# Second and third gate of a decoder trunk as seven products of half-size blocks

## What is computed

```python
b_ga, b_gb, b_gc = jnp.split(b_gate, N_BRANCH, axis=-1)
merged = (jax.nn.sigmoid(ga + b_ga) * jnp.einsum('bsw,wd->bsd', y_a, w_branch[0])
          + jax.nn.sigmoid(gb + b_gb) * jnp.einsum('bsw,wd->bsd', y_b, w_branch[1])
          + jax.nn.sigmoid(gc + b_gc) * jnp.einsum('bsw,wd->bsd', y_c, w_branch[2]))
mixed = jnp.einsum('bsd,de->bse', merged, w_o)
x = _layer_norm(ALPHA * x + mixed, ln1_g, ln1_b)
h = jnp.square(jax.nn.relu(jnp.einsum('bsd,df->bsf', x, w_up)))
x = _layer_norm(ALPHA * x + jnp.einsum('bsf,fd->bsd', h, w_down), ln2_g, ln2_b)
```

## Time and profile before

| | us |
|---|---|
| median of 3 runs | 835.32 (833.45 to 835.56) |
| the profiled execution | 836.42 |
| its span, first to last instruction | 834.6 |
| PE busy | 819.2 |
| DVE busy | 504.1 |
| ACT busy | 348.7 |
| POOL busy | 20.8 |
| the three gates, on PE | 252.09 to 447.93 |

### The profile page before, as it was taken

How to read it: one execution, slowest core, us unless ns; L and a number is a source line. 1 busy time by engine, 2 the same in 40 slices (tenths; PEclk the granted TensorE clock), 3 DMA queues, 4 the chain that set the end, 5 groups by cost and what they waited for, 6 DMA issues and landing times.

```text
span 834.6 us, 10182 instructions
## 1 busy us (share of the span) xinstructions
PE 819.2 (98%) x4111; PEld 695.7 (83%) x4111; DVE 504.1 (60%) x560; ACT 348.7 (42%) x393; POOL 20.8 (2%) x30
## 2 busy tenths in 40 slices
PE   8999999999999999999999999999999999999994
PEld 7989988889888888888888889888888888888883
DVE  3647735567364424414428685885669566947698
ACT  4539343484334223232225035653545345435430
POOL 1110100000001000000000010000000000000000
PEclk9999999999999999999999999999999999999998
DMA  9641313312212322323833407017301810270002
GB/s 304 201 152 52 101 51 97 105 50 83 68 66 90 117 82 100 101 101 101 302 101 99 153 7 247 0 51 252 102 0 53 301 51 0 84 270 1 0 1 101
DMA packets 68215, 87.52 MB, mean 105 GB/s; under 512 B 1581, under 2 KB 51798, under 8 KB 68182
## 3 DMA queue, kind: packets, MB, share of 16 engines
q1 hardware_dynamic: 68182, 87.06, 31.0%
HBM read 84.96 MB, written 2.10 MB: 104 GB/s over the span
## 4 chain that ended last, share of the span: by engine, by line
PE 94%; DVE 4%; issue 1%; DMA 1%; DVEq 0%; SPq 0%; ACT 0%
PE bank L1272 30%; PE bank L1274 30%; PE bank L1273 30%; DVE two L1172 1%; DVE two L1184 1%; DMA two<-in_mem_dram 1%; PE bank L1486 0%; PE bank L1436 0%; PE bank L1554 0%; PE bank L1407 0%; PE bank L1299 0%; DVE two L1189 0%; DVE w_lo L761 0%; DVE decay L1178 0%; DVE smx L1178 0%
## 5 line engine op out<-in xcount | busy, mean ns | idle before, releaser
L1272 PE MATMUL bank<-x_hi,w_hi 128*128 128x512 f32 (+1 forms) x704 | 268.4, 381 | 0.0
L1273 PE MATMUL bank<-x_lo,w_hi 128*128 128x512 f32 (+1 forms) x704 | 267.2, 380 | 0.0
L1274 PE MATMUL bank<-x_hi,w_lo 128*128 128x512 f32 (+1 forms) x704 | 267.2, 379 | 0.0
L756 DVE TENSOR_TENSOR w_lo<-raw,w_hi 128x2048 fp32r<-128x2048 f32 x40 | 91.5, 2291 | 107.7 <-ACT w_hi L474 107.5
L1274 PEld LDWEIGHTS bank<-x_hi,w_lo 128*128 128x128 f32 x704 | 132.4, 188 | 25.1
L1272 PEld LDWEIGHTS bank<-x_hi,w_hi 128*128 128x128 f32 x704 | 132.4, 188 | 24.6
L1273 PEld LDWEIGHTS bank<-x_lo,w_hi 128*128 128x128 f32 x704 | 132.5, 188 | 24.5
L1272 PE MATMUL bank<-w_hi,y_hi 128*128 128x512 f32 (+1 forms) x320 | 121.5, 380 | 0.4 <-DVE two L1172 0.4
L1274 PE MATMUL bank<-w_hi,y_lo 128*128 128x512 f32 (+1 forms) x320 | 121.1, 378 | 0.0
L1273 PE MATMUL bank<-w_lo,y_hi 128*128 128x512 f32 (+1 forms) x320 | 121.1, 378 | 0.0
L474 ACT ACTIVATE w_hi<-raw 128x2048 fp32r<-128x2048 f32 x40 | 76.4, 1915 | 41.7 <-PE bank L1274 36.8
(11 more groups left out here) (182 smaller groups left out, 834.2 us busy)
## 6 DMA issues: line engine op xcount, KB each, us to landing
raw<-in_w_in_dram SPq DMA_DIRECT2D x28, 1024.0 KB, 5.0
raw<-in_w_up_dram SPq DMA_DIRECT2D x16, 1024.0 KB, 8.8
small<-in_w_down_dram SPq DMA_DIRECT2D x12, 1024.0 KB, 7.0
raw<-in_w_branch_dram SPq DMA_DIRECT2D x6, 1024.0 KB, 5.1
raw<-in_w_o_dram SPq DMA_DIRECT2D x4, 1024.0 KB, 5.1
raw<-in_w_down_dram SPq DMA_DIRECT2D x4, 1024.0 KB, 4.7
two<-in_x_dram SPq DMA_DIRECT2D x2, 1024.0 KB, 11.0
small<-in_w_mem_v_dram SPq DMA_DIRECT2D x2, 1024.0 KB, 11.8
```

The costliest lines, as they stand in the source:

```text
L756: dve.tensor_tensor(w_lo[:, slot, :], raw[:, r, :], w_hi[:, slot, :].bitcast(F32), ALU.subtract)\
L1272: pe.matmul(dst, a[0], b[0], start=first, stop=False, skip_group_check=goes_on)
L1273: pe.matmul(dst, a[0], b[1], start=False, stop=False, skip_group_check=goes_on)
L1274: return pe.matmul(dst, a[1], b[0], start=False, stop=last, skip_group_check=goes_on)
```

## The change

The gates' loop is written out. The first gate is computed as before, in the order gate slabs 0 and 1, both branch slabs, gate slabs 2 and 3; its products open `merged`, so the clearing goes. The second and third gate (x times a 1024 x 1024 block) are each made of seven products m1 to m7, over half the tokens (256), half of the 1024 inputs (4 blocks) and half of the outputs (512). The operands are three blocks of x as they are (m1, m2, m4) and four sums of blocks (m5, m6, m7, m3), formed once by VectorE during the first gate and split into parts; and three blocks of weights as loaded (m1, m2, m3), with four sums (m5, m6, m4, m7), which VectorE forms in the raw buffers. The branch slabs come seventh and ninth in the order. The quarter results z11, z12, z22 are formed in SBUF from two or more products (ScalarE copies one out of PSUM, VectorE adds the next), while others accumulate in PSUM; z21 is read from PSUM.

Two more raw buffers lie over rows 0 to 3 of y_hi and y_lo, free once the first branch is used. Half results lie in rows 1, 2, 4 and 5 of `two`, sums of x in rows 0 and 3 of `two` and in small[:, 4096:9216].

The core of the diff, by engine. SyncE (`gate_load(i, name)` loads one slab of gate i, i = 3 is w_o; `split_of` waits until that slab's low part is made):

```diff
+            split_of(0, "g2")
+            gate_load(1, "m1")
+            split_of(0, "g3")
+            gate_load(1, "m2")
+
+            sp.wait_ge(tile_done, GATE_ROUND * MAIN + 12)
+            gate_load(1, "c")
+            gate_load(1, "m3")
+            split_of(1, "m6")
+            sp.wait_ge(gate_block_summed, block_summed(1, "m4"))
+            gate_load(1, "b1")
...
+            gate_load(3, 0)
+            split_of(2, "m7")
+            gate_load(2, "b0")
+            split_of(2, "m4")
+            gate_load(3, 1)
+            sp.wait_ge(slab_lo, S_OUT + 1)
+            gate_load(3, 2)
+
+            sp.wait_ge(merge_done, merged_at(2, KD - 1))
+            sp.wait_ge(gate_done, gate_made(2, "m4", 1))
             sp.dma_start(resid, x_t).then_inc(x_again, 16)
+            sp.wait_ge(slab_lo, S_OUT + 2)
+            gate_load(3, 3)
             for n, v in enumerate((ln1_g, ln1_b, ln2_g, ln2_b)):
                 sp.dma_start(ln_par[:, n, :], v.to_broadcast((P, D))).then_inc(ln_landed, 16)
-            for e in range(2):
-                for h in range(2):
-                    load(S_OUT + 2 * e + h, h, wout[:, 4 * h:4 * h + 4, e * WID:(e + 1) * WID], 4)
```

ScalarE (for i = 1, 2; `nexts(p)` is the slab four places on, `product(i, name)` waits until that product is made):

```diff
+                if i == 2:
+                    gate_hi(2, "m6", product(1, "b0"))
+                gate_copy(i, "m1", "z11", 1.0)
+                gate_hi(*nexts(1), product(i, "m1"))
+                gate_hi(*nexts(2), product(i, "m2"))
+                gate_opens(i, "z11")
+                gate_copy(i, "m5", "z22", 1.0)
+                gate_hi(*nexts(3), product(i, "m5"))
+                gate_copy(i, "m6", "z12", -1.0)
+                gate_hi(*nexts(4), product(i, "m6"))
+                gate_hi(*nexts(5), product(i, "m3"))
+                gate_opens(i, "z12")
+                gate_hi(*nexts(6), product(i, "m7"))
+                gate_opens(i, "z22")
+                gate_hi(*nexts(7), product(i, "b1"))
+                if i == 2:
+                    merged_parts(0)
+                gate_opens(i, "z21")
+                gate_hi(*nexts(8), product(i, "m4"))
             merged_parts(1)
-            hi(S_OUT + 3, 2, OUT_ROUND * MAIN)
+            gate_hi(3, 3, product(2, "b0"))
```

VectorE (for i = 1, 2):

```diff
+                gate_lo(i, "m6")
+                block_sum(i, "m4")
+                gate_lo(i, "m3")
+                block_sum(i, "m7")
+                gate_sums(i, "z11")
+                gate_lo(i, "m7")
+                gate_lo(i, "b1")
+                gate_lo(i, "m4")
+                gate_sums(i, "z12")
+                gate_lo(i, "b0")
+                gate_sums(i, "z22")
+                if i == 1:
+                    gate_lo(2, "m1")
+                else:
+                    gate_lo(3, 0)
+                gate_merge(i, 1)
+                if i == 1:
+                    gate_lo(2, "m2")
+                    block_sum(2, "m5")
+                    gate_lo(2, "m5")
+                    block_sum(2, "m6")
+                else:
+                    gate_lo(3, 1)
+                    merged_parts(0)
+                    gate_lo(3, 2)
+                gate_merge(i, 0)
             merged_parts(1)
-            lo(S_OUT + 2, 3)
-            lo(S_OUT + 3, 2)
+            gate_lo(3, 3)
```

TensorE (the order is LATER_GATE):

```diff
+LATER_GATE = ("m1", "m2", "m5", "m6", "m3", "m7", "b1", "m4", "b0")
...
+            def gate_product(i, name):
+                s = gate_slab(i, name)
+                slab(s)
+                if i == 1 and name in ("m6", "m7", "m5", "m3"):
+                    pe.wait_ge(x_sum_split, ("m6", "m7", "m5", "m3").index(name) + 1)
+                opens = name in ("m1", "m2", "m5")
+                for t in range(4):
+                    if t % 2 == 0:
+                        gate_ready(i, name, t // 2)
+                    for k in range(4):
+                        mm = three(gate_acc(name, t), w_part(s % 4, k * WID + t * P, P),
+                                   both(x_form_hi[name], x_form_lo[name], ALL, k), opens and k == 0 and t % 2 == 0,
+                                   k == 3, not opens or t % 2 == 1)
+                    if t % 2:
+                        mm.then_inc(gate_done, 1)
```

More of the change, by code:

```diff
@@ L352, in _ @@
                     load(half * N_PROJ + (S_PROJ + j), j % 2, win_256[:, :, ds(n, 1), :], KD)
-            with sp.Fori(0, 3) as i:
-                for h in range(2):
[L355 to L359, removed]
@@ L606, in _, with gate_hi @@
                         .then_inc(hgrn_hi, 1)
[L609 to L629, removed]
+            def gate_hi(i, name, earlier):
+                earlier()
+                if i == 3:
+                    s, p, src = S_OUT + name, OUT_PLACE[name], name
+                    act.wait_ge(place_landed[p], landing(3, name))
+                else:
+                    s = gate_slab(i, name)
+                    if i == 0 or name in ("m1", "m2", "m3", "b1", "b0"):
+                        p = place_of(i, name)
+                        act.wait_ge(place_landed[p], landing(i, name))
+                    else:
+                        p = PLACE[i][dict(m5="m1", m6="m1", m4="m2", m7="m3")[name]]
+                        act.wait_ge(gate_block_summed, block_summed(i, name))
+                act.activation(w_hi[:, s % 4, :], gate_raw[p], ACT.Copy).then_inc(slab_hi, 1)
@@ L639, in _ @@
-            gates(2, True)
-            hi(S_OUT + 2, 3)
+            gate_hi(0, "b0", tiles(-2))
+            gate_hi(0, "b1", tiles(0))
+            act.wait_ge(branch_split, 8)
+            first_opens(0)
+            first_opens(1)
+            gate_hi(0, "g2", tiles(2))
+            x_sum_high("m6", 1)
+            first_opens(2)
+            first_opens(3)
+            gate_hi(0, "g3", tiles(4))
+            x_sum_high("m7", 2)
+            x_sum_high("m5", 2)
+            gate_hi(1, "m1", tiles(8))
@@ L1003, in _, with gate_lo @@
                 assert chain[0] == CHAIN_HALF, chain
[L1006 to L1024, removed]
+            def gate_lo(i, name):
+                if i == 3:
+                    s, p = S_OUT + name, OUT_PLACE[name]
+                else:
+                    s = gate_slab(i, name)
+                    p = place_of(i, dict(m5="m1", m6="m1", m4="m2", m7="m3").get(name, name))
+                dve.wait_ge(slab_hi, s + 1)
+                low_of(w_lo[:, s % 4, :], gate_raw[p], w_hi[:, s % 4, :]).then_inc(slab_lo, 1)
@@ new lines, in gate_merge @@
+            def gate_merge(i, f):
+                for c in range(4):
+                    k = 4 * (1 - f) + c
+                    row = merged[:, k, :].rearrange("p (a t) -> p a t", a=2)
+                    g = gate_tile(f, c)
+                    dve.wait_ge(gate_opened, opened(i, "z22" if f else "z21", c))
+                    dve.wait_ge(gate_done, gate_made(i, "b%d" % f, c))
+                    src = bank[BRANCH_BANK[c]].rearrange("p (a t) -> p a t", a=2)
+                    dve.tensor_tensor(g, g, src, ALU.mult).then_inc(branch_read, 1)
+                    if i == 1 and k < 4:
+                        main_copied(dve, GATE_ROUND, 4 + k)
+                    else:
+                        dve.wait_ge(merge_done, merged_at(i - 1, k))
+                    dve.wait_ge(branch_read, KD * (i - 1) + k + 1)
+                    dve.tensor_tensor(row, row, g, ALU.add).then_inc(merge_done, 1)
@@ L1094, in _ @@
                 if b == TB - 1:
-                    lo(S_MLP, 0)
-                    lo(S_MLP + 1, 1)
+                    for n in (S_MLP, S_MLP + 1):
+                        dve.wait_ge(slab_hi, n + 1)
+                        low_of(w_lo[:, n % 4, :], raw[:, n % 2, :], w_hi[:, n % 4, :]).then_inc(slab_lo, 1)
                 mixed(b, 1)
@@ L1511, in _, with first_gate @@
                 feature_tile(rnd, 15, 3, 1)
[L1513 to L1530, removed]
+            def first_gate(name):
+                s = gate_slab(0, name)
+                slab(s)
+                n = int(name[1])
+                if name[0] == "g":
+                    t0 = 2 * n if n < 2 else 12 + 2 * (n - 2)
+                    for c in range(2):
+                        feature_tile(GATE_ROUND, t0 + c, s % 4, c)
+                    return
+                pe.wait_ge(branch_split, 8)
+                for c in range(4):
+                    dst = begin(GATE_ROUND, 4 + 4 * n + c)
+                    for k in range(HEADS):
+                        mm = three(dst, w_part(s % 4, k * WID + c * P, P), both(y_hi, y_lo, ALL, k),
+                                   k == 0, k == HEADS - 1)
+                    mm.then_inc(tile_done, 1)
@@ new lines, in branch_product @@
+            def branch_product(i, f):
+                s = gate_slab(i, "b%d" % f)
+                slab(s)
+                for c in range(4):
+                    if f == 0:
+                        pe.wait_ge(branch_read, KD * (i - 1) + c + 1)
+                    elif BRANCH_BANK[c] < 2:
+                        pe.wait_ge(gate_summed, summed(i, "z11", BRANCH_BANK[c]))
+                    elif i == 1:
```

(7 more changed lines are left out.)

307 lines of the change are left out of this document (279 added, 28 removed).

## The result

| | before | changed |
|---|---|---|
| median of 20 runs, us | 835.08 | 836.51 |
| lowest to highest | 833.45 to 836.38 | 835.04 to 838.66 |
| profiled execution | 836.42 | 835.04 |
| its span | 834.6 | 833.1 |

The ratio is 1.0022, 95% interval 1.0015 to 1.0028. So the changed kernel is slower by 0.22%. That is less than the 0.3% that the prediction takes for no change, though the interval excludes 1. Forecast: 836.2.

The account below looks back on a forecast made before the run. TensorE's stream of matmuls was taken as the bound (PE busy 819.2 of 834.6 us). 836.42 - 6.40 (gates) + 5.5 (stall) + 1.8 (clock) = 837.3, less 1.10 gives 836.2 us; range 831.5 to 839.5.

Parts of the forecast that it names:

- Rate of 256-token matmuls: Later two gates: 256-token matmuls take 0.120 us each, so each gate saves 3.2 us, 6.4 us together.
- The Trainium skill's formula: Isolated matmul gap of N/2.4 + 2.5 ns; would save 9.5 us in two gates; the prediction used the trace's figures instead.
- VectorE's and ScalarE's new work is hidden: Later gates: VectorE 44.9 us and ScalarE 27.5 us in 62.1 us, costed at nothing, as is the first gate's extra work.
- the edge at the refill of the weight slots: Later gates: refilling a slab's slot has 17.3 us of cover and needs 12.0 us at worst.
- What is late next: After the gates: x issued at 443.4 behind the last merge, fourth w_o slab behind it; PE stands still 5.5 us.
- No second wait: First layer norm: x1 ready some 7 us after the ln loads; PE first asks 11 us after the stall's end.
- The clock: Behind the w_o stall: clock falls from 2.4 to 1.2 GHz, costing 1.8 us, bounds 0 and 2.4.
- The 4 us at the lower level: Start of trace: 256-token matmuls 0.213 us apart instead of 0.120 for some 4 us, used to price the clock's fall.
- the even choice that 0.36 against 0.28 made of it: Stall of 4 to 7 us at the w_o slab: chance 0.36 with the clock's fall, 0.28 without.
- the w_o slab did not share the engines with x: Rival, load not late enough: slab shares with x, lands about 2.5 us sooner, stall 3.0 us, 831.9 us; chance 0.14.
- the loads did not crawl: Rival: x load and slab behind it at 290 GB/s, stall 8.7 us, clock down 1.8, 839.4 us; chance 0.14.
- the gates did not starve: Rival in the gates: late z sum on VectorE holds PE, a few us per event; chance 0.08 together with slow matmuls.

Follow-up runs that it names:

- e8: Changed kernel with fourth w_o slab, ln vectors and two rows of x loaded early, plus four extra VectorE passes per later gate: 828.65 us, 0.9926 to before.
- e6: e1 with VectorE making the low part twice for all nine slabs of each later gate: 836.29 us, ratio 1.0011 to the kernel before.
- e1: Changed kernel with the fourth w_o slab loaded once its raw buffer is free, ahead of the last-merge wait: 827.62 us, ratio 0.9917 to before.
- e2: Changed kernel with the fourth w_o slab ahead of x, both still behind the last merge: 832.28 us, ratio 0.9966 to the kernel before.
- e10: The changed kernel itself, unaltered, measured again beside the early-slab version on one chip: 837.04 us, ratio 1.0031 to the kernel before.
- e4: Kernel before, gates untouched, with x, the fourth w_o slab and the ln vectors moved behind the last merge: 845.22 us, ratio 1.0115.

## Why the prediction was right

The sum came out term by term, the clock's term partly by luck.
- *Rate of 256-token matmuls.* 0.120 us forecast, gates of 62.12 us found: the saving is 6.3 us, 6.4 forecast. The Trainium skill's formula (TensorE: Matmul & The Clock Gate, section Back-to-back issue gap), which would have given 9.5, is not borne out by this kernel either.
- *VectorE's and ScalarE's new work is hidden.* VectorE 42.6 to 43.5 us busy per later gate, 44.9 forecast, no PE gap; e8 shows it with 9 us more, e6 where it ends. The prediction looked for the edge at the refill of the weight slots. The one that e6 found is a hand-over out of PSUM, the copy of m5, which the prediction took for safe because a copy is short: ScalarE makes it in order, behind work that waits for VectorE. In the changed kernel it was done at 394.63 for a use at about 399.6.
- *What is late next.* The last merge ended 1.75 us after the gates (1.68 forecast) and x was issued 1.78 us after them (1.9), slab at hand 10.6 after the x issue (10.2), stop 5.75 (5.5).
- *No second wait.* Right for the changed kernel. But the some 4 us to spare (ready 7 us after the ln loads, wanted 11 us after the stall; 3.3 us in the profile, x1 ready at 464.86 and wanted at 468.21) belong to a kernel that has just stood still. Once the stall is gone (e1) it is 0.5 us, and in e2 it is gone.
- *The clock.* The size was right, 1.97 against 1.8, but the argument for it was weaker than it looked. The 4 us at the lower level came from the start of the trace, where the earlier trace rows show only matmuls of 256 tokens; PE also ran eight transposes ahead of them in 1.57 us, 0.2 us each (the changed kernel's profile has the same eight in 0.79 us), and the clock column reads 1.00 there, so the level is read from the rate alone. Behind the stops the time was 4.0 us here, 3.1 in e10 and 6.2 in e4, so that 4 is one value of several. Whether it would fall rested on one figure, the 5.2 us between the last matmul and the fall at the end of the trace, just under the stop of 5.5. In one profile the fall came 2.95 us into the stop, in e10 only 0.3 us before its end; but of the 26 measured executions of the changed kernel all but one have a mean granted clock of 0.993 or less, and that one has 0.994. So it was not the even choice that 0.36 against 0.28 made of it.

The rivals: the w_o slab did not share the engines with x (e2: swapped, it came 5 us sooner), the loads did not crawl in the changed kernel, though in e4 they took 1.4 us more, and the gates did not starve.

## What to carry to other kernels

When a change reuses buffers, list what was loaded into them early and ask for each load what now stands ahead of it in its queue. Here a slab whose own buffer was free 14 us sooner (e1 issues it at 426.51, the changed kernel at 440.88) was late only because it stood behind a wait and a load that it did not need; that order cost 7.7 us, more than seven products for eight saved. And price a stop of TensorE at more than its length: where the clock fell with it, these runs paid 1.3 to 3 us on top.

## What the runs showed that was not expected

**How soon the clock falls.** Stops and falls, in us: changed kernel, stop at 449.56, fall 2.95 later; e4, stop at 457.91, fall 3.1 later; e2, stop at 463.83, fall 2.5 later; e6, stop at 401.31, fall 4.7 later. The changed kernel's second profile (e10) stopped at 449.77 for 5.76 us, and there the clock held almost until PE began again:

```profile
454.00:455.00 1.00, 0.00 (x0) 0.00 (x0) 1.00 (x1) 0.45 (x1) 0.00 (x0) 1.00 1.03 422
455.00:456.00 1.00, 0.47 (x1) 0.47 (x2) 0.47 (x1) 0.00 (x0) 0.00 (x0) 0.62 0.57 234
...
458.00:459.00 1.00, 1.00 (x5) 0.77 (x4) 0.28 (x1) 0.00 (x0) 0.00 (x0) 0.68 0.95 281
```

0.62 over 455 to 456 puts the fall at 455.2, 5.5 us after the stop and 0.3 us before the next matmul; it rose at 458.6. So the time from stop to fall is not fixed: in two executions of one kernel it was 2.95 and 5.5 us. The time at the lower level after PE went on was 2.8 us in e6, 3.1 in e10, 3.4 in e2, 4.0 in the changed kernel and 6.2 in e4.

**The start of the span moves the total.** The same prologue put the last projection tile at 246.65 before and at 243.72 in the changed kernel, and between in the others. The rows of before, show matmuls 0.213 us apart until about 13 us; in the changed kernel's profile they were at 0.120 already at 8 us:

```profile
8.03 0.28 PE L1628 MATMUL bank<-y_lo,w_hi 128*128 128x256 f32 x1
8.15 0.28 PE L1629 MATMUL bank<-y_hi,w_lo 128*128 128x256 f32 x1
```

By the fifteenth such matmul (13.49 before, 10.45 in the changed kernel) the lead is 3.0 us, and from there to the last projection tile it hardly changes. 0.213 us is the spacing of the same matmuls in e6 at 407 us, where the granted clock reads 0.50:

```profile
407.00:408.00 1.00, 1.00 (x6) 1.00 (x6) 1.00 (x1) 1.00 (x1) 0.00 (x0) 0.50 0.00 0
```

So PE worked at the lower level there for longer in one execution than in the other. This is read from the rate alone: the clock column reads 1.00 over that stretch in both profiles. It explains why the changed kernel's profiled execution is 1.4 us faster than the profiled one before while its median is 1.4 us slower. Two single executions of this kernel can't be compared to better than 3 us by their totals; the rest from a fixed matmul on can, to about half a microsecond (581.65 and 582.03 for one kernel, 589.38 and 588.97 for the other).
